# The opening of a hybrid decoder block: how x is normalised, turned and handed to the first projections

## Chip, cores, metric

One core of a Trainium2 chip. The metric is the device time of one execution in microseconds; the median of the runs is given. The hardware profiler recorded one further execution.

## What is computed

The reference is one pre-norm residual layer in float32 for 512 tokens of width 1024, with 16 learned meta tokens put in front (528 tokens in all). What matters here is its first step and what consumes it:

```python
def rmsnorm(x, g):
    y = x * rsqrt(mean(x * x, axis=-1) + 1e-6)
    return y * g

h = concatenate([zeros(PAD), meta_tokens, x])     # PAD only aligns blocks; masked out
u = rmsnorm(h, norm_g)
hq, hf, hi, hz, aq, ak, av, az, ga, gb = split(u @ w_in)   # ten 1024-wide projections
# branch A: gated linear recurrence on (hq, hf, hi), RMSNorm, silu(hz) gate
# branch B: differential softmax attention on (aq, ak, av), RMSNorm, silu(az) gate
m = sigmoid(ga) * (oA @ w_branch_a) + sigmoid(gb) * (oB @ w_branch_b)
out = rmsnorm(h + m @ w_out, final_g)             # meta tokens dropped
```

TensorE contracts over partitions, so `u` has to be brought into channel-major form (channels on the partitions, tokens in the columns) before the first projection. Matmuls of the projections are made of three products: each operand is split into a rounded high part (`_hi`, type fp32r) and the remainder (`_lo`), and hi·hi, hi·lo and lo·hi are summed in PSUM (function `three`, lines 379 to 383).

## The kernel before

x is taken in tiles of 128 tokens (0 to 3) and one tile of 16 meta tokens (index `CH` = 4), in the order `X_ORDER = (0, 1, CH, 2, 3)`. Each goes through these steps, and each step is a function called by hand in the program of its engine, so the order of the calls is the order of the work:

1. ScalarE squares it with a sum over the row (`square_x`, L717 to L724).
2. VectorE makes the mean plus eps (`mean_x`, L980), POOL raises it to −0.5 (L367): `rstd`.
3. VectorE multiplies the tile by `rstd` (one per token) and by the norm weight `g_in` in one instruction (`norm_x`, L977). `g_in` holds norm_g on all 128 partitions, a 512 KB broadcast.
4. TensorE turns its eight 128x128 blocks with the identity (`turn_x`, L386 to L401) into two PSUM banks.
5. ScalarE copies them out, rounded, to `uT_hi` (L734), and VectorE subtracts to get `uT_lo` (L996). The meta tile has shorter forms (L396, L730, L991).

Weights come in units of 128 output channels by 1024 (512 KB). A unit is loaded into one of two buffers, ScalarE makes its high part (`convert_hi`, L247) and VectorE its low part (`convert_lo`, L252); unit u is loaded once unit u−2 has been converted (`lo_ready`). The first two units are used in four pieces (`half_section`, L454): half 0 takes the meta tokens and tiles 0 and 1, half 1 tiles 2 and 3. 24 matmuls make one piece. `half_section(s, half)` waits for `lo_ready` of its unit and for `u_ready_lo`. Then come whole sections (`groups`), of which section 2, with 264-column matmuls, is the first. After them eight heads, each with its eight projections and its recurrence and attention laid between them, then gates, branch projections, the output projection and the last norm.

TensorE's order at the start: turn tiles 0 and 1, wait for `rows_ready` (three small loads into `rows_in`: lower-bound logits and two head norm weights) and transpose those 18 rows (L468), turn the meta tile and tile 2, half section (0,0), turn tile 3, half sections (1,0), (0,1), (1,1). VectorE waits for that transpose (`pe_pre`) and copies it (L1009) between its work on tiles 0 and 1.

DMAs are issued by SP (x tiles 0 and 1, weight unit 0, x tiles 2 and 3, unit 1, `rows_in`, four tables, then the further units) and by ScalarE (identity, norm_g, meta tokens). Engines work their queues in order, and wait on semaphores where shown.

Of the kernel before, what the change touches and what calls it, by code (L numbers as in the profile page):

```python
# [43 lines left out]

X_ORDER = (0, 1, CH, 2, 3)

# [46 lines left out]
def build(nc, x, meta_tokens, norm_g, w_in, lb_logits, hg_norm_g, da_lambda, da_norm_g,  # L93
# [22 lines left out]
    x_in, o2 = at("x_in", [P, NT, D], F32, region_o)  # L116
    g_in, o2 = at("g_in", [P, D], F32, o2)
    x_sq, o2 = at("x_sq", [P, D], F32, o2)
# [31 lines left out]
    gate_a, o = at("gate_a", [P, SEQ], F32, o)  # L150
    gate_b, o = at("gate_b", [P, SEQ], F32, o)
    kT, o = at("kT", [P, TOK], F32, o)
    qT, o = at("qT", [P, SEQ], F32, o)
# [31 lines left out]

    lbt = cols(2 * HEADS + 2)
    f_mul, f_neg, f_add, e_0, e_1, e_m = (cols(HEADS) for _ in range(6))
    gain_a, gain_b, neg_lam, lam2, warm = cols(1), cols(1), cols(1), cols(2), cols(NT)
    ss, ms, rstd, half_neg, ss2 = (cols(NT) for _ in range(5))
# [4 lines left out]
    def bank(i):  # L194
        return ps[:, i, :]
# [7 lines left out]
    def level_bank(e):  # L203
# [16 lines left out]
    x_squared, x_ms, x_rstd, x_normed, x_turned = (sem(n) for n in (  # L220
        "x_squared", "x_ms", "x_rstd", "x_normed", "x_turned"))

    sec_taken = sem("sec_taken")
# [61 lines left out]
    with block:  # L285

        @block.sync
        def _(sp):
# [89 lines left out]
        def _(pe):  # L378
# [6 lines left out]

            def turn_x(n):  # L386

                i = X_ORDER[n]
                pe.wait_ge(x_normed, n + 1)
                if i == CH:  # L390
                    pe.wait_ge(v_pre, 1)
                elif n > 2:
                    pe.wait_ge(u_ready_lo, n - 2)
                for k in range(KT):
                    if i == CH:
                        t = pe.transpose(bank(3)[:, k * META:(k + 1) * META], x_in[0:META, CH, k * P:(k + 1) * P],  # L396
                                         ident[0:META, 0:META])
                    else:
                        t = pe.transpose(bank(4 + 2 * (i % 2) + k // 4)[:, (k % 4) * P:(k % 4 + 1) * P],
                                         x_in[:, i, k * P:(k + 1) * P], ident[:, :])  # L400
                t.then_inc(x_turned, 1)  # L401


            def recurrent_out(s, b):
# [296 lines left out]
        @block.scalar  # L701
        def _(act):
            act.dma_start(ident[:, :], c_ident).then_inc(ident_in, 16)
            act.dma_start(g_in[:, :], norm_g.to_broadcast([P, D])).then_inc(norm_in, 16)
            act.dma_start(x_in[0:META, CH, :], meta_tokens).then_inc(meta_in, 16)

            act.wait_ge(g_pre, 1)
            act.activation(warm, half_neg, ACT.Square)

# [6 lines left out]

            def square_x(n):  # L717
                i = X_ORDER[n]
                m = P if i < CH else META
                act.wait_ge(*((x_loaded[i], 16) if i < CH else (meta_in, 16)))  # L720
                if n > 0:
                    act.wait_ge(x_squared, n)
                act.activation(x_sq[0:m, :], x_in[0:m, i, :], ACT.Square, accum_out=ss[0:m, i:i + 1]) \
                    .then_inc(x_squared, 1)  # L724

            def turned_x(n):
                i = X_ORDER[n]
                act.wait_ge(x_turned, n + 1)
                if i == CH:
                    act.activation(uT_hi[:, :, 0:META], bank(3)[:, 0:KT * META].rearrange("p (k t) -> p k t", k=KT),  # L730
                                   ACT.Copy).then_inc(u_ready_hi, 1)
                    return
                for g in range(2):
                    ins = act.activation(uT_hi[:, 4 * g:4 * g + 4, META + i * P:META + (i + 1) * P],  # L734
                                         bank(4 + 2 * (i % 2) + g).rearrange("p (k t) -> p k t", k=4), ACT.Copy)
                ins.then_inc(u_ready_hi, 1)
# [12 lines left out]
            turned_x(4)  # L749
            convert_hi(act, 2, 2, 2)  # L750
# [211 lines left out]
        def _(dve):  # L962
# [6 lines left out]

            def norm_x(n):  # L970

                i = X_ORDER[n]
                m = P if i < CH else META
                dve.wait_ge(x_rstd, n + 1)
                if n == 0:
                    dve.wait_ge(norm_in, 16)
                dve.scalar_tensor_tensor(x_in[0:m, i, :], x_in[0:m, i, :], rstd[0:m, i:i + 1], g_in[0:m, :],  # L977
                                         ALU.mult, ALU.mult).then_inc(x_normed, 1)

            def mean_x(n):  # L980
                i = X_ORDER[n]
                m = P if i < CH else META
                dve.wait_ge(x_squared, n + 1)
# [3 lines left out]
            def turned_x(n):  # L987
                i = X_ORDER[n]
                dve.wait_ge(u_ready_hi, n + 1)
                if i == CH:  # L990
                    dve.tensor_tensor(uT_lo[:, :, 0:META], bank(3)[:, 0:KT * META].rearrange("p (k t) -> p k t", k=KT),  # L991
                                      uT_hi[:, :, 0:META].bitcast(F32), ALU.subtract).then_inc(u_ready_lo, 1)
                    return
                for g in range(2):
                    lo, hi = (a[:, 4 * g:4 * g + 4, META + i * P:META + (i + 1) * P] for a in (uT_lo, uT_hi))
                    ins = dve.tensor_tensor(lo, bank(4 + 2 * (i % 2) + g).rearrange("p (k t) -> p k t", k=4),  # L996
                                            hi.bitcast(F32), ALU.subtract)
                ins.then_inc(u_ready_lo, 1)

            mean_x(0)  # L1000
            mean_x(1)
            norm_x(0)
            norm_x(1)
            mean_x(2)
            norm_x(2)
            turned_x(0)
            mean_x(3)
            dve.wait_ge(pe_pre, 1)
            pre(dve.tensor_copy(lbt, bank(3)[:, 256:256 + 2 * HEADS + 2]))  # L1009
            turned_x(1)  # L1010
            norm_x(3)
            convert_lo(dve, 0, 0)
            turned_x(2)
            mean_x(4)
            norm_x(4)
            turned_x(3)
            convert_lo(dve, 1, 1)
            turned_x(4)
            convert_lo(dve, 2, 2)
# [352 lines left out]
```

## Time and profile before

| | us |
|---|---|
| median of 3 runs (758.33 to 758.58) | 758.37 |
| the profiled execution | 758.68 |
| its span | 756.5 |

The profiled execution lasted 2.2 us longer than its span, which runs from the first to the last recorded activity. In the rows, PE is TensorE's matmuls, PEld its weight loads, DVE VectorE, ACT ScalarE, POOL GpSimd and SP the engine that issues DMAs; a q behind the name is the engine's sequencer. Start times are counted from the start of the span. "L381" is line 381 of the kernel.

### The profile page before, as it was taken

Reading aid. Unit: us, or ns where it says so; the run is one execution under the profiler, and the core shown is the slowest. Engines: PE = TensorE matmul, PEld = TensorE weight load, DVE = VectorE, ACT = ScalarE, POOL = GpSimd, SP = SyncE. Lnnn points to the kernel's source line nnn. Section 1 sums busy time; section 2 is a strip of 40 time slices with the busy share of each in tenths; the row PEclk is TensorE's granted clock in tenths of the full one; section 3 lists DMA queues with packets and bytes.
Section 4 is the critical chain, followed back from the end, with each engine's and each line's share of the span. In section 5 each row is a group of like instructions: output and inputs, shape, how many; then the busy total and the mean of one; then the engine's idle time right before and its main releaser. Section 6 shows DMA issues by size and latency. Waiting matters only on the chain.

```text
span 756.5 us, 13114 instructions
## 1 busy us (share of the span) xinstructions
PE 737.0 (97%) x4729; PEld 656.1 (87%) x4729; DVE 462.5 (61%) x973; ACT 284.0 (38%) x580; POOL 22.9 (3%) x34
## 2 busy tenths in 40 slices
PE   3999999999999999999999999999999999999996
PEld 2998999999899899989989989998888888888885
DVE  4668669668767856966876786695643433333352
ACT  5414443542552444255145235425522222232232
POOL 2000000000000000000000000000000000000001
PEclk9999999999999999999999999999999999999999
DMA  7421220230122123023012212302323223332602
GB/s 253 126 70 56 84 84 16 68 111 28 55 83 83 55 81 85 0 83 111 28 55 83 83 33 82 107 1 85 112 85 112 83 84 111 96 98 86 246 29 111
DMA packets 105416, 63.24 MB, mean 84 GB/s; under 512 B 2067, under 2 KB 100901, under 8 KB 105397
## 3 DMA queue, kind: packets, MB, share of 16 engines
q1 hardware_dynamic: 105076, 62.33, 27.4%
q10 hardware_dynamic: 320, 0.66, 0.3%
q8 instruction: 12, 0.20, 0.1%
q14 instruction: 8, 0.06, 0.0%
HBM read 60.88 MB, written 2.10 MB: 83 GB/s over the span
## 4 chain that ended last, share of the span: by engine, by line
PE 96%; SPq 1%; issue 1%; DMA 1%; DVE 0%; ACT 0%; POOLq 0%; POOL 0%; DVEq 0%; ACTq 0%
PE ps L381 26%; PE ps L382 26%; PE ps L383 26%; PE ps L502 3%; PE ps L571 3%; PE ps L600 2%; PE ps L488 1%; PE ps L591 1%; PE ps L578 1%; PE ps L601 1%; PE ps L536 1%; PE ps L535 1%; PE ps L518 1%; PE ps L543 1%; DMA rows_in<-in_da_norm_g 1%
## 5 line engine op out<-in xcount | busy, mean ns | idle before, releaser
L381 PE MATMUL ps<-uT_hi,w_hi 128*128 128x512 f32 (+3 forms) x960 | 323.9, 337 | 0.0
L382 PE MATMUL ps<-uT_lo,w_hi 128*128 128x512 f32 (+3 forms) x960 | 308.6, 321 | 0.0
L383 PE MATMUL ps<-uT_hi,w_lo 128*128 128x512 f32 (+3 forms) x960 | 308.0, 321 | 0.0
L383 PEld LDWEIGHTS ps<-uT_hi,w_lo 128*128 128x128 f32 x960 | 181.0, 189 | 13.9
L381 PEld LDWEIGHTS ps<-uT_hi,w_hi 128*128 128x128 f32 x960 | 181.8, 189 | 12.1
L382 PEld LDWEIGHTS ps<-uT_lo,w_hi 128*128 128x128 f32 x960 | 181.7, 189 | 11.1
L252 DVE TENSOR_TENSOR w_lo<-w_raw,w_hi 128x1024 fp32r<-128x1024 f32 x104 | 126.2, 1220 | 95.9 <-ACT w_hi L247 95.1
L247 ACT ACTIVATE w_hi<-w_raw 128x1024 fp32r<-128x1024 f32 x104 | 110.0, 1057 | 87.5 <-PE ps L383 84.3
L809 ACT ACTIVATE e<-ps,small 128x144 f32<-128x144 f32 (+2 forms) x48 | 23.0, 483 | 47.7 <-DVE small L1194 47.7
L1140 DVE TENSOR_REDUCE small<-sq 128x4 f32<-128x512 f32 x16 | 11.0, 686 | 40.1 <-ACT sq L798 40.1
L371 POOL TENSOR_TENSOR small<-small 128x4 f32<-128x4 f32 x16 | 16.1, 1007 | 512.5 <-DVE small L1141 512.5
L502 PE MATMUL ps<-qq,sq 128*128 128x128 f32 x192 | 29.9, 278 | 0.0
L502 PEld LDWEIGHTS ps<-qq,sq 128*128 128x128 f32 x192 | 27.1, 190 | 3.0
L1131 DVE COPY_PREDICATED aa<-masks,ps 128x256 f32<-128x256 uint8 x56 | 29.0, 518 | 0.0
L1191 DVE TENSOR_REDUCE small<-ps 128x2 f32<-128x288 f32 (+3 forms) x32 | 26.9, 841 | 0.0
L834 ACT ACTIVATE kT_hi<-kT 128x528 fp32r<-128x528 f32 x8 | 5.2, 646 | 57.5 <-DVE kT L1177 57.5
L381 PE MATMUL ps<-oa_hi,w_hi 128*128 128x512 f32 x64 | 24.9, 390 | 0.0
L382 PE MATMUL ps<-oa_lo,w_hi 128*128 128x512 f32 x64 | 24.9, 389 | 0.0
L383 PE MATMUL ps<-oa_hi,w_lo 128*128 128x512 f32 x64 | 24.9, 389 | 0.0
L381 PE MATMUL ps<-ob_hi,w_hi 128*128 128x512 f32 x64 | 24.9, 389 | 0.0
L382 PE MATMUL ps<-ob_lo,w_hi 128*128 128x512 f32 x64 | 24.9, 389 | 0.0
L383 PE MATMUL ps<-ob_hi,w_lo 128*128 128x512 f32 x64 | 24.9, 389 | 0.0
(191 smaller groups left out, 1020.4 us busy)
## 6 DMA issues: line engine op xcount, KB each, us to landing
w_raw<-in_w_in SPq DMA_DIRECT2D x80, 512.0 KB, 3.7
w_raw<-in_w_branch_a SPq DMA_DIRECT2D x8, 512.0 KB, 3.5
w_raw<-in_w_branch_b SPq DMA_DIRECT2D x8, 512.0 KB, 3.6
w_raw<-in_w_out SPq DMA_DIRECT2D x8, 512.0 KB, 3.9
x_in<-in_x SPq DMA_DIRECT2D x4, 512.0 KB, 7.8
x_res<-in_x SPq DMA_DIRECT2D x4, 512.0 KB, 6.4
out<-y_out SPq DMA_DIRECT2D x8, 256.0 KB, 2.2
rope<-in_c_rope SPq DMA_DIRECT2D x1, 528.0 KB, 6.0
```

Of the source, the lines that this page charges most:

```text
L247: act.activation(w_hi[:, slot, :], w_raw[:, slot % RAW, :], ACT.Copy).then_inc(hi_ready, 1)
L252: eng.tensor_tensor(w_lo[:, slot, :], w_raw[:, slot % RAW, :], w_hi[:, slot, :].bitcast(F32), ALU.subtract).then_inc(lo_ready, 1)
L371: pool.tensor_tensor(rstd[:, 0:CH], ms[:, 0:CH], half_neg[:, 0:CH], ALU.pow).then_inc(rstd_ready, 1)
L381: pe.matmul(dst, w[0], rhs[0], start=start, stop=False, skip_group_check=True)
L382: pe.matmul(dst, w[0], rhs[1], start=False, stop=False, skip_group_check=True)
L383: return pe.matmul(dst, w[1], rhs[0], start=False, stop=stop, skip_group_check=True)
L502: mm = pe.matmul(walk(dst, i * P // 2, (P, 2), (m, P // (2 * m)), (1, m)), k_mix[:, i, :], walk(qq[:, i * P:], m, (HALF - m, 2), (2 * m, P ...
L571: pe.matmul(bank(B_S + comp)[:, 0:n - at_k], q[half[comp], q_b], k[half[comp], at_k:n], start=i == 0, stop=False, skip_group_check=True)
L600: pe.matmul(dst, pT[:, j, :], v_b[:, j, :], start=(j == 0), stop=False)
L809: ins = act.activation(e[:, 0:n], bank(B_S + comp)[:, 0:n], ACT.Exp, bias=nb[:, comp:comp + 1], scale=SCALE, accum_out=lsum[:, comp:comp + 1])
L1131: dve.copy_predicated(dst, mask, got).then_inc(lvl_taken, 1)
L1191: chain(dve.tensor_reduce(mx, ps[:, B_S:B_S + 2, 0:n], AX.X, ALU.max))
```

## The change

- `X_ORDER` becomes `(CH, 0, 1, 2, 3)`: the meta tile is first. Its squares are taken by VectorE instead of ScalarE (`meta_sq`, with the sum).
- `g_in` holds norm_g on 16 partitions only (64 KB), for the meta tile, which is still multiplied by `rstd` and norm_g in one instruction. For all other tiles norm_g is applied later: it is also loaded as 8 rows of 128 (`g_rows`, 4 KB), transposed by TensorE and copied to the 8 columns `g_col`, and used as the per-partition scale when PSUM is copied out, by ScalarE (`scale=g_col`) and by VectorE (a SCALAR_TENSOR_TENSOR in place of the TENSOR_TENSOR). Both norm_g loads are issued by SP behind x1; ScalarE issues meta first, then the identity.
- Tiles 0 and 1 are not normalised on VectorE. VectorE multiplies the identity by `rstd` into a diagonal matrix (128x128), and TensorE multiplies the raw block with this diagonal, an fp32 matmul in place of a transpose. Tiles 2 and 3 are still multiplied by `rstd` on VectorE (a TENSOR_SCALAR) and transposed with the identity.
- PSUM is laid out by channel block: two tiles (256 columns) of two k share a bank, and PSUM is copied out in pieces of 256 columns, two k at a time, with a semaphore count for each pair.
- TensorE's order: ten matmuls of a zero tile with itself (`WARM`), the transpose of norm_g, diagonal turn of tile 0, meta turn, diagonal turn of tile 1, half section (0,0), turns of tiles 2 and 3, half section (1,0), transpose of `rows_in`, half sections (0,1) and (1,1).
- The zero tile, the diagonals and `g_rows` lie in buffers that the heads use later.

The core of the diff:

```diff
-X_ORDER = (0, 1, CH, 2, 3)
+X_ORDER = (CH, 0, 1, 2, 3)
+WARM = 10
...
                 if i == 1:
+                    sp.dma_start(g_rows, norm_g.rearrange("l (k p) -> (l k) p", p=P)).then_inc(g_loaded, 16)
+                    sp.dma_start(g_in[:, :], norm_g.to_broadcast([META, D])).then_inc(norm_in, 16)
                     section(0, 0, 0, 0)
...
+            pool.memset(zeros, 0.0).then_inc(zeros_ready, 1)
             pool.memset(half_neg, -0.5).then_inc(g_pre, 1)
...
+            def scale_and_turn(i):
+                pe.wait_ge(diag_ready, i + 1)
+                for k in range(KT):
+                    mm = pe.matmul(turned(k, i), x_in[:, i, k * P:(k + 1) * P], diag[:, i, :], start=True, stop=True)
+                    if i == 1 and k % 2 == 1:
+                        mm.then_inc(x_turned, 1)
+
+            def turn_x(i):
+                pe.wait_ge(x_normed, i)
+                for k in range(KT):
+                    if i == 2:
+                        pe.wait_ge(u_ready_lo, k // 2 + 1)
+                    t = pe.transpose(turned(k, i), x_in[:, i, k * P:(k + 1) * P], ident[:, :])
+                    if i == 3 and k % 2 == 1:
+                        t.then_inc(x_turned, 1)
...
             def half_section(s, half):
                 pe.wait_ge(lo_ready, s + 1)
-                pe.wait_ge(u_ready_lo, (3, NT)[half])
+                pe.wait_ge(u_ready_lo, (4, 8)[half])
...
+            pe.wait_ge(zeros_ready, 1)
+            for _ in range(WARM):
+                pe.matmul(bank(2)[:, P:2 * P], zeros, zeros, start=True, stop=True)
             pe.wait_ge(ident_in, 16)
-            turn_x(0)
-            turn_x(1)
+            pe.wait_ge(g_loaded, 16)
+            pe.transpose(bank(2)[:, 0:KT], g_rows, ident[0:KT, 0:KT]).then_inc(g_turned, 1)
+            scale_and_turn(0)
+            turn_meta()
+            scale_and_turn(1)
+            half_section(0, 0)
+            turn_x(2)
+            turn_x(3)
+            half_section(1, 0)
             pe.wait_ge(rows_ready, 48)
             pe.transpose(bank(3)[:, 256:256 + 2 * HEADS + 2], rows_in[:, :], ident[0:2 * HEADS + 2, 0:2 * HEADS + 2]) \
                 .then_inc(pe_pre, 1)
-            turn_x(2)
-            turn_x(3)
-            half_section(0, 0)
-            turn_x(4)
-            half_section(1, 0)
             half_section(0, 1)
             half_section(1, 1)
...
+            def turned_hi(half):
+                for j in range(KT // 2):
+                    act.wait_ge(x_turned, KT // 2 * half + j + 1)
+                    for k in (2 * j, 2 * j + 1):
+                        ins = act.activation(uT_hi[:, k, META + half * HALF:META + (half + 1) * HALF],
+                                             ps[:, 4 + j, k % 2 * HALF:(k % 2 + 1) * HALF], ACT.Copy,
+                                             scale=g_col[:, k:k + 1])
+                    ins.then_inc(u_ready_hi, 1)
             square_x(0)
             square_x(1)
+            convert_hi(act, 0, 0, 1)
+            meta_turned_hi()
+            act.wait_ge(g_ready, 1)
+            turned_hi(0)
             square_x(2)
-            turned_x(0)
             square_x(3)
-            turned_x(1)
-            convert_hi(act, 0, 0, 1)
-            turned_x(2)
-            square_x(4)
-            turned_x(3)
             convert_hi(act, 1, 1, 1)
-            turned_x(4)
+            turned_hi(1)
             convert_hi(act, 2, 2, 2)
...
+            def diagonal(i):
+                dve.wait_ge(x_rstd, i + 2)
+                dve.tensor_scalar(diag[:, i, :], ident[:, :], rstd[:, i:i + 1], None, ALU.mult).then_inc(diag_ready, 1)
...
+            dve.wait_ge(meta_in, 16)
+            meta_x = x_in[0:META, CH, :]
+            dve.scalar_tensor_tensor(meta_sq[:, :], meta_x, 1.0, meta_x, ALU.mult, ALU.mult,
+                                     accum_out=ss[0:META, CH:CH + 1]).then_inc(meta_squared, 1)
             mean_x(0)
+            dve.wait_ge(g_turned, 1)
+            dve.tensor_copy(g_col, bank(2)[:, 0:KT]).then_inc(g_ready, 1)
+            dve.wait_ge(norm_in, 16)
+            dve.wait_ge(x_rstd, 1)
+            dve.scalar_tensor_tensor(meta_x, meta_x, rstd[0:META, CH:CH + 1], g_in[:, :], ALU.mult, ALU.mult) \
+                .then_inc(x_normed, 1)
+            dve.wait_ge(ident_in, 16)
             mean_x(1)
+            diagonal(0)
             mean_x(2)
+            diagonal(1)
+            convert_lo(dve, 0, 0)
+            dve.wait_ge(meta_hi, 1)
+            dve.tensor_tensor(uT_lo[:, :, 0:META], bank(3)[:, 0:KT * META].rearrange("p (k t) -> p k t", k=KT),
+                              uT_hi[:, :, 0:META].bitcast(F32), ALU.subtract)
+            dve.wait_ge(g_ready, 1)
+            turned_lo(0)
+            mean_x(3)
+            norm_x(2)
+            mean_x(4)
+            norm_x(3)
+            convert_lo(dve, 1, 1)
+            turned_lo(1)
             dve.wait_ge(pe_pre, 1)
             pre(dve.tensor_copy(lbt, bank(3)[:, 256:256 + 2 * HEADS + 2]))
```

## Rows read from the trace of the kernel before

**Rows 1.** The page: busy time, granted clock in 40 slices, one group of section 5

```profile
PE 737.0 (97%) x4729; PEld 656.1 (87%) x4729; DVE 462.5 (61%) x973; ACT 284.0 (38%) x580; POOL 22.9 (3%) x34
...
PEclk9999999999999999999999999999999999999999
...
PE 96%; SPq 1%; issue 1%; DMA 1%; DVE 0%; ACT 0%; POOLq 0%; POOL 0%; DVEq 0%; ACTq 0%
...
L252 DVE TENSOR_TENSOR w_lo<-w_raw,w_hi 128x1024 fp32r<-128x1024 f32 x104 | 126.2, 1220 | 95.9 <-ACT w_hi L247 95.1
```

**Rows 2.** Timeline of TensorE: start us, us, engine, line, operation, count [idle before]

```profile
9.83 3.65 PE L399 MATMUL ps<-ident,x_in 128*128 128x128 f32 x16 [9.83 <-DVE x_in L977]
15.21 0.29 PE L468 MATMUL ps<-ident,rows_in 18*128 18x18 f32 x1 [1.73 <-DMA rows_in<-in_da_norm_g]
15.86 1.00 PE L396 MATMUL ps<-ident,x_in 16*128 16x16 f32 x8 [0.36 <-DVE small L1009]
18.15 1.97 PE L399 MATMUL ps<-ident,x_in 128*128 128x128 f32 x8 [1.29 <-DVE x_in L977]
19.77 0.58 PE L381 MATMUL ps<-uT_hi,w_hi 128*128 128x272 f32 x1
20.15 0.43 PE L382 MATMUL ps<-uT_lo,w_hi 128*128 128x272 f32 x1
...
22.60 0.28 PE L381 MATMUL ps<-uT_hi,w_hi 128*128 128x272 f32 x1
...
24.11 1.04 PE L399 MATMUL ps<-ident,x_in 128*128 128x128 f32 x8
...
33.51 0.28 PE L381 MATMUL ps<-uT_hi,w_hi 128*128 128x264 f32 x1
```

**Rows 3.** Chain of waits in order of time: start us, us, what

```profile
4.89 4.42 SPq L308
...
9.73 5.43 DMA rows_in<-in_da_norm_g
...
52.86 0.45 PE ps L502 x4
```

**Rows 4.** Timeline of ScalarE, square of tile 0

```profile
4.68 1.06 ACT L723 ACTIVATE x_sq<-x_in 128x1024 f32<-128x1024 f32 x1 [1.02 <-DMA x_in<-in_x]
5.64 0.19 ACT L723 ACTIVATION_READ_ACCUMULATOR x_sq<-x_in 128x1 f32 x1
```

**Rows 5.** Stretches: window, its length, engines' busy us, clock, DMA share, GB/s

```profile
10.50:12.00 1.50, 1.50 (x9) 1.40 (x9) 0.96 (x2) 0.20 (x1) 0.46 (x1) 1.00 1.01 387
```

**Rows 6.** DMA issues to 60 us: KB each, median us from issue to landing

```profile
w_raw<-in_w_in SPq DMA_DIRECT2D x9, 512.0 KB, 3.7
...
g_in<-in_norm_g ACTq DMA_DIRECT2D x1, 512.0 KB, 7.0
```

**Rows 7.** Timeline of VectorE: the meta tile's mean and norm, the copy of rows_in

```profile
11.33 0.13 DVE L984 TENSOR_SCALAR small<-small 16x1 f32<-16x1 f32 x1
12.11 1.27 DVE L977 SCALAR_TENSOR_TENSOR x_in<-x_in,small,g_in 16x1024 f32<-16x1024 f32 x1 [0.65 <-POOL small L367]
...
15.53 0.18 DVE L1009 COPY small<-ps 128x18 f32<-128x18 f32 x1 [0.89 <-PE ps L468]
```

**Rows 8.** Groups by form, ScalarE and VectorE: busy us, mean ns | idle before

```profile
L786 ACT ACTIVATE z_g<-ps,small 128x512 f32<-128x512 f32 x16 | 10.8, 673 | 0.0
L785 ACT ACTIVATE th_z<-ps 128x512 f32<-128x512 f32 x16 | 9.3, 584 | 40.4 <-PE ps L383 40.4
L823 ACT ACTIVATE pT<-ps 128x256 f32<-128x256 f32 x8 | 3.1, 383 | 1.9 <-PE ps L594 1.9
L1105 DVE TENSOR_TENSOR kk<-kk,tt 128x256 f32<-128x256 f32 x40 | 17.0, 424 | 11.1 <-PE ps L502 8.1 <-DVE e L1173 1.5 <-DVE e L1166 1.5
L1205 DVE TENSOR_SCALAR e<-e,small 128x528 f32<-128x528 f32 x8 | 3.9, 490 | 0.0
L1205 DVE TENSOR_SCALAR e<-e,small 128x144 f32<-128x144 f32 x8 | 2.3, 288 | 0.0
```

More of the change, by code:

```diff
@@ L116, in build @@
     x_in, o2 = at("x_in", [P, NT, D], F32, region_o)
-    g_in, o2 = at("g_in", [P, D], F32, o2)
+    g_in, o2 = at("g_in", [META, D], F32, o2)
+    meta_sq, o2 = at("meta_sq", [META, D], F32, o2)
     x_sq, o2 = at("x_sq", [P, D], F32, o2)
@@ L151, in build @@
     gate_b, o = at("gate_b", [P, SEQ], F32, o)
+    diag, zeros, g_rows = st[:, 0:2, :], on[:, 0, :], og[0:KT, 0:P]
     kT, o = at("kT", [P, TOK], F32, o)
@@ L184, in cols @@
         return small[:, taken[0] - n:taken[0]]
-    lbt = cols(2 * HEADS + 2)
+    lbt, g_col = cols(2 * HEADS + 2), cols(KT)
     f_mul, f_neg, f_add, e_0, e_1, e_m = (cols(HEADS) for _ in range(6))
-    gain_a, gain_b, neg_lam, lam2, warm = cols(1), cols(1), cols(1), cols(2), cols(NT)
+    gain_a, gain_b, neg_lam, lam2, warm = cols(1), cols(1), cols(1), cols(2), cols(1)
     ss, ms, rstd, half_neg, ss2 = (cols(NT) for _ in range(5))
@@ L221, in build @@
         "x_squared", "x_ms", "x_rstd", "x_normed", "x_turned"))
+    zeros_ready, g_loaded, g_turned, g_ready = (sem(n) for n in ("zeros_ready", "g_loaded", "g_turned", "g_ready"))
+    meta_squared, meta_turned, meta_hi, diag_ready = (sem(n) for n in (
+        "meta_squared", "meta_turned", "meta_hi", "diag_ready"))
     sec_taken = sem("sec_taken")
@@ L383, in three, with turn_meta, turned @@
                 return pe.matmul(dst, w[1], rhs[0], start=False, stop=stop, skip_group_check=True)
[L386 to L393, printed above, removed]
-                for k in range(KT):
[L395 to L401, printed above, removed]
+            def turn_meta():
+                pe.wait_ge(x_normed, 1)
+                for k in range(KT):
+                    t = pe.transpose(bank(3)[:, k * META:(k + 1) * META], x_in[0:META, CH, k * P:(k + 1) * P],
+                                     ident[0:META, 0:META])
+                t.then_inc(meta_turned, 1)
+            def turned(k, i):
+                return ps[:, 4 + k // 2, (k % 2) * HALF + (i % 2) * P:(k % 2) * HALF + (i % 2 + 1) * P]
+            def scale_and_turn(i):
[12 more added lines that the diff above has]
+                        t.then_inc(x_turned, 1)
             def recurrent_out(s, b):
@@ L702, in _ @@
         def _(act):
+            act.dma_start(x_in[0:META, CH, :], meta_tokens).then_inc(meta_in, 16)
             act.dma_start(ident[:, :], c_ident).then_inc(ident_in, 16)
-            act.dma_start(g_in[:, :], norm_g.to_broadcast([P, D])).then_inc(norm_in, 16)
-            act.dma_start(x_in[0:META, CH, :], meta_tokens).then_inc(meta_in, 16)
             act.wait_ge(g_pre, 1)
-            act.activation(warm, half_neg, ACT.Square)
+            act.activation(warm, half_neg[:, 0:1], ACT.Square)
             act.sem_inc(og_ready, 2)
@@ L715, in _, with square_x @@
             act.sem_inc(gate_taken, 4)
[L717 to L736, printed above, removed]
+            def square_x(i):
+                act.wait_ge(x_loaded[i], 16)
+                if i > 0:
+                    act.wait_ge(x_squared, i)
+                act.activation(x_sq[:, :], x_in[:, i, :], ACT.Square, accum_out=ss[:, i:i + 1]).then_inc(x_squared, 1)
@@ new lines, in meta_turned_hi @@
+            def meta_turned_hi():
+                act.wait_ge(meta_turned, 1)
+                act.activation(uT_hi[:, :, 0:META], bank(3)[:, 0:KT * META].rearrange("p (k t) -> p k t", k=KT),
+                               ACT.Copy).then_inc(meta_hi, 1)
+            def turned_hi(half):
[6 more added lines that the diff above has]
+                    ins.then_inc(u_ready_hi, 1)
@@ L968, in pre @@
                 return own[0]
[L970 to L978, printed above, removed]
             def mean_x(n):
@@ L982, in mean_x @@
                 m = P if i < CH else META
-                dve.wait_ge(x_squared, n + 1)
+                dve.wait_ge(*((x_squared, n) if n else (meta_squared, 1)))
                 dve.tensor_scalar(ms[0:m, i:i + 1], ss[0:m, i:i + 1], 1.0 / D, EPS, ALU.mult, ALU.add) \
                     .then_inc(x_ms, 1)
[L987 to L998, printed above, removed]
@@ L1000, in _, with norm_x, turned_lo @@
-            mean_x(0)
+            def diagonal(i):
+                dve.wait_ge(x_rstd, i + 2)
+                dve.tensor_scalar(diag[:, i, :], ident[:, :], rstd[:, i:i + 1], None, ALU.mult).then_inc(diag_ready, 1)
+            def norm_x(i):
+                dve.wait_ge(x_rstd, i + 2)
+                dve.tensor_scalar(x_in[:, i, :], x_in[:, i, :], rstd[:, i:i + 1], None, ALU.mult) \
+                    .then_inc(x_normed, 1)
+            def turned_lo(half):
+                for j in range(KT // 2):
+                    dve.wait_ge(u_ready_hi, KT // 2 * half + j + 1)
+                    for k in (2 * j, 2 * j + 1):
+                        lo, hi = (a[:, k, META + half * HALF:META + (half + 1) * HALF] for a in (uT_lo, uT_hi))
+                        ins = dve.scalar_tensor_tensor(lo, ps[:, 4 + j, k % 2 * HALF:(k % 2 + 1) * HALF],
+                                                       g_col[:, k:k + 1], hi.bitcast(F32), ALU.mult, ALU.subtract)
+                    ins.then_inc(u_ready_lo, 1)
@@ L1005, in _ @@
+            mean_x(3)
             norm_x(2)
-            turned_x(0)
-            mean_x(3)
+            mean_x(4)
+            norm_x(3)
+            convert_lo(dve, 1, 1)
+            turned_lo(1)
             dve.wait_ge(pe_pre, 1)
             pre(dve.tensor_copy(lbt, bank(3)[:, 256:256 + 2 * HEADS + 2]))
[L1010 to L1017, printed above, removed]
@@ L1018, in _ @@
-            turned_x(4)
             convert_lo(dve, 2, 2)
```

3 lines of the change are left out of this document (1 added, 2 removed).

## The prediction

> **What bounds the kernel now.** I read the page first: TensorE is busy in 97% of the span, and the chain that ended last lies 96% on it [rows 1]. The other engines wait for it, so the only time to be won or lost by an edit of the opening is the time at which TensorE begins its unbroken run, and the rate at which it starts. I therefore went to the timeline of TensorE [rows 2]. The reader is to see four stretches there: nothing until 9.83; 16 transposes to 13.48; a hole until 15.21, which the transpose of rows_in ends; then small pieces until 18.15, from which it never stops again. The first weight matmul starts at 19.77, and the groups of section 2 (the first 264-column one) at 33.51. From there on both kernels have the same instructions, so I forecast the shift of this one moment. The chain of waits [rows 3] says why the hole is there: rows_in was issued late, its first DMA held SP for 4.42 us, and the last landed 5.43 us after issue. Behind that wait stood two more turns on TensorE and the copy on VectorE.
>
> The rate is the second thing. The page grants full speed in every slice (a 9, [rows 1]), and still the 272-column matmuls start every 0.223 us from 20.15 to 22.60 (eleven steps, the last already shorter), and every 0.126 us from 22.60 to 24.11 (twelve). 272 columns in 0.223 us is the 1.2 GHz level, in 0.126 us the 2.4 GHz level. The granted clock of the profile does not show this step; the pitch does. The 16 transposes at 9.83 (0.228 us each) ran at the low level too; the eight at 24.11 took half as long (1.04 for 1.97 us).
>
> **The opening after the change.** Loads first. SP issues x0, x1, then the two small norm_g loads (4 KB and 64 KB), and the 512 KB broadcast of norm_g is gone from ScalarE's queue. x0 was used at 4.68 [rows 4]. At 387 GB/s [rows 5] the 0.52 MB of x1 take 1.35 us more, so x1 is there near 6.0, and norm_g right behind, say 6.1. That is the first term: **norm_g at 6.1.** The bounds: 5.7, if meta and ident fit in earlier, and, by the 7.0 us from issue to landing of the old broadcast [rows 6] on an issue at 1.6, 8.6.
>
> TensorE's zero matmuls start after POOL's first memset, about 1.0. An fp32 128-column matmul is two records here: the chain has four records of L502 in 0.45 us [rows 3], 0.225 us a matmul at the high level, double at the low one. Ten take 4.5 us, to 5.5 at the latest, before norm_g is there: they cost nothing. Nor do the other edits of the first 6 us, all of them under the loads: one memset more on POOL, the squares of the meta tile on VectorE (1.27 [rows 7] and a power, from some 3.7 to 5.8), one DMA issue less on ScalarE; without that cover the squares would add 1.3. Then the queue of VectorE decides, because it is in order and mean_x of x0 stands behind the whole meta norm:
> - transpose of norm_g and its copy, as those of rows_in from 15.21 [rows 2] to 15.53 + 0.18 [rows 7]: 0.5 together, to 6.6;
> - meta norm, one instruction of 1.27, at 12.11 [rows 7]: 7.85;
> - mean, power on POOL, next instruction: 0.78, from 11.33 to 12.11 [rows 7]: 8.65. The other edges of this step (x0 squared near 5.9) are long done;
> - the diagonal, 128 columns, no row of its own; the 144-column TENSOR_SCALAR takes 0.29 [rows 8]: scale_and_turn(0) starts at **8.9**.
>
> TensorE then has 8 fp32 matmuls in place of 8 transposes: 1.8 us at the high level, to 10.7. The eight meta transposes took 1.00 at 15.86, taken unchanged: 11.7. scale_and_turn(1): 1.8, to 13.5, with the first pair of k handed on at 12.15. The diagonal for x1 and lo(0) lie on VectorE meanwhile (0.78 + 0.3, then 1.22 [rows 1], from 8.8 to 11.1), the weights' hi on ScalarE after x1's square; both are covered, by more than 0.5 us.
>
> Now the evictions are the bound, not TensorE (0.45 a pair). The 256-column activation out of PSUM takes 0.383, and I take starts to overlap by 0.1; a per-partition scale adds 0.09 (0.673 with, 0.584 without, at 512 columns, [rows 8]). That is 0.36 to 0.37 a start, so 0.72 a pair, four pairs: 12.15 to 15.05. VectorE's two 256-column operations (0.424 each, 0.35 apart [rows 8], a tensor pair standing for the new form) follow the last pair: 0.8. Half section (0,0) starts at **15.9**; bounds 14.9 (0.28 a start and g at 5.7) and 18.4 (g at 8.6).
>
> The sum to the start of section 2, against 19.77 to 33.51 of before:
> - first weight matmul 15.9 for 19.77: −3.9;
> - its 24 matmuls at 0.126, 3.0 us, for 4.34 (19.77 to 24.11): −1.3, if the clock is up;
> - two turns of x stand behind it, where there was one: +0.9;
> - rows_in's transpose, now within the run: +0.3.
> Together −4.0.
>
> Does the second half keep up? ScalarE after 15.05: two squares with their accumulator reads (4.68 to 5.83, 1.15 each [rows 4]), hi(1) of the same size 1.06: 18.4. VectorE: mean and power 0.78 after the first square, 17.0; norm_x(2) now is a TENSOR_SCALAR. 144 columns take 0.288 and 528 take 0.490, 0.53 ns a column [rows 8], so 1024 make 0.75 (an estimate), not the 1.27 of the norm of before [rows 7]: 17.75; the same once more: 19.2; lo(1) 1.22: 20.4. TensorE needs x3 at 19.8 and lo(1) at 20.7: covered by 0.6 and 0.3. The four pairs of x2 and x3 then run on ScalarE from 20.0 to 22.9 and on VectorE to 23.7, and TensorE asks for them at 23.8. That is a tie; I add 0.2 for it. **−3.8 us.** If norm_x took 1.27 after all, 0.8 more would be lost here, net of the cover of 0.3 to 0.6: I keep that for the range. Later, w2 to w6 are asked for by lo_ready, which moves with the rest.
>
> The profiled execution took 758.68 for a span of 756.5, and the median of the runs is 758.37. −3.8 gives 754.9 against the profiled execution and 754.6 against the median; I forecast 754.6, 0.5% faster.
>
> **A rule that speaks against this.** The rows [rows 2] show TensorE at the low level after an idle opening, and show one rise, at 22.5, after unbroken work from 18.15; no row shows a fall, because there is no idle stretch later. In the new order it stands still, but for one small transpose, from 5.5 to 8.9, and again from 13.5 to 15.9. The Trainium skill (TensorE: Matmul & The Clock Gate, section on the HAM clock gate) says that the engine goes back to half rate when left idle, so that warming up early can be lost by the time the data is there. No row shows it. If it holds here, rival 1 is the case.
>
> **Rivals.**
> 1. *The clock is low where it counts.* The zeros do not raise it, or the wait until 8.9 loses it. Then scale_and_turn(0) takes 3.65, to 12.55, the meta turn is done at 13.55, and if the rise comes 4.35 us after 8.9, as from 18.15, scale_and_turn(1) is fast: first pair 14.0, half section at 17.7, 1.8 later: −2.0, 756.4. With a rise after 2.7 us, as counted from the first weight matmul at 19.77, it would be −2.4. If it is lost between 13.5 and 15.9 instead, the 1.3 us of the half section are not won: −2.5. For it: the two idle stretches. Against: the zero matmuls last as long (4.5) as the run that raised it before.
> 2. *norm_g lands late as well:* 1.5 us later (7.6) and the clock low: −0.5, 757.9. This is "no change". For it: the spread of the landings, where 512 KB took 3.7 us in the median of the weights and 7.0 in the opening [rows 6].
> 3. *Slower: the gate on norm_g.* Before, norm_g was needed by one instruction; now VectorE's whole queue stands behind g_turned, x0's power included. A tiny load is not a quick one: rows_in went from 4.89 to 15.16, 10.3 us [rows 3]. If norm_g issued at 1.6 lands at 11.9, everything is 5.8 us later, 2.0 us net, and with the clock low (TensorE idle since 5.5) 3.8: 760.4 to 762.2. It decides from a landing at 9.9. Against: rows_in stood behind four tiles of x and two weight units and a DMA that held SP, norm_g stands behind x0 and x1 only.
>
> **How the numbers follow.** Forecast 58%, rival 1 25%, rival 2 10%, rival 3 7%. A measurement of this kernel can tell about 0.2%, 1.5 us, from no change. Faster: the forecast, and nearly all of rival 1, 0.81; same: rival 2 and a rest, 0.13; slower: 0.06. The range: below, 753.6 (the first bound, 14.9, for 15.9); above, 757.0, which holds rival 1 and a g at 7.6 with the clock up.
>
> **What would show it.** TensorE's timeline: zeros from 1.0 to about 5 with a pitch that halves before their end; L502-like pitch of 0.11 a record in the scaled turns, from 8.9; first weight matmul at 15.9 with a pitch of 0.126 from the start; the first 264-column matmul at 29.7; no idle time of TensorE afterwards beyond 0.3. A scaled turn at 0.22 a record speaks for rival 1, a VectorE copy of norm_g after 7.5 for rivals 2 and 3. I am wrong if TensorE idles elsewhere in the opening, above all ahead of half section (1,0) or (0,1), or if section 2 starts 3 us earlier and the time does not follow.

## The result and the profile after

The change made the kernel slower. Median 760.43 us (759.67 to 762.51, 11 runs) against 758.58 us of the kernel before in the same runs (758.02 to 759.25): ratio 1.0029, 95% interval 1.0021 to 1.0037. That is 1.85 us by the medians. The forecast was 754.6 with a range of 753.6 to 757.0. The profiled execution has a span of 758.4 (756.5 before): +1.9.

The page after, as in [rows 1]: TensorE is as dominant as before.

```profile
PE 743.3 (98%) x4766; PEld 662.0 (87%) x4766; DVE 462.6 (61%) x984; ACT 284.9 (38%) x586; POOL 22.1 (3%) x35
...
PE 96%; DVE 1%; issue 1%; DMA 1%; ACT 0%; POOL 0%; SPq 0%; POOLq 0%; DVEq 0%; ACTq 0%
```

The timeline of TensorE after, which answers to [rows 2] (single 272-column matmuls thinned out; `on`, `st` and `og` are the buffers that are lent to the zero tile, the diagonals and `g_rows`):

```profile
1.00 4.64 PE L484 MATMUL ps<-on 128*128 128x128 f32 x20 [1.00 <-POOL on L367]
7.28 0.24 PE L487 MATMUL ps<-ident,og 8*128 8x8 f32 x1 [1.64 <-DMA og<-in_norm_g]
10.01 3.78 PE L409 MATMUL ps<-st,x_in 128*128 128x128 f32 x16 [2.49 <-DVE st L999]
13.72 0.71 PE L398 MATMUL ps<-ident,x_in 16*128 16x16 f32 x8
14.36 2.05 PE L409 MATMUL ps<-st,x_in 128*128 128x128 f32 x16
19.48 0.36 PE L390 MATMUL ps<-uT_hi,w_hi 128*128 128x272 f32 x1 [3.07 <-DVE uT_lo L1011]
...
20.69 0.42 PE L390 MATMUL ps<-uT_hi,w_hi 128*128 128x272 f32 x1
20.91 0.43 PE L391 MATMUL ps<-uT_lo,w_hi 128*128 128x272 f32 x1
...
24.08 1.93 PE L418 MATMUL ps<-ident,x_in 128*128 128x128 f32 x16
25.76 0.36 PE L390 MATMUL ps<-uT_hi,w_hi 128*128 128x256 f32 x1
...
29.64 0.35 PE L390 MATMUL ps<-uT_hi,w_hi 128*128 128x256 f32 x1 [0.63 <-DVE uT_lo L1011]
...
35.39 0.28 PE L390 MATMUL ps<-uT_hi,w_hi 128*128 128x264 f32 x1
```

The first 264-column matmul starts at 35.39, 1.88 later than at 33.51: the whole loss, and nothing behind it adds to it. The reader is to see three things. The first scaled turn (L409, 16 records) takes 3.7 us and the second, of the same instructions, about 1.9 (3.78 and 2.05 with the last record's tail): between them TensorE's rate doubled. The half section starts 3.07 us after the turns are done, waiting for VectorE. And its matmuls start every 0.125 us until 20.69 and every 0.23 afterwards: the rate was lost again. Stretches of TensorE (length, busy, granted clock, DMA share, GB/s):

```profile
10.00:15.00 5.00, 4.99 (x29) 1.00 1.08 356
15.00:20.00 5.00, 1.93 (x17) 1.00 0.36 96
20.00:25.00 5.00, 5.00 (x31) 0.66 0.07 19
```

0.66 is a mean of the two levels, 2.4 and 1.2 GHz. The low level of 10.01 to 13.7 is not in the column (1.00); only the pitch of the records shows it.

VectorE's and ScalarE's timeline after, for [rows 7] and [rows 4]:

```profile
7.55 0.17 DVE L1021 COPY small<-ps 128x8 f32<-128x8 f32 x1 [2.11 <-PE ps L487]
7.66 1.27 DVE L1024 SCALAR_TENSOR_TENSOR x_in<-x_in,small,g_in 16x1024 f32<-16x1024 f32 x1
8.86 0.13 DVE L994 TENSOR_SCALAR small<-small 128x1 f32<-128x1 f32 x1
9.67 0.28 DVE L999 TENSOR_SCALAR st<-ident,small 128x128 f32<-128x128 f32 x1 [0.67 <-POOL small L376]
...
16.11 3.23 DVE L1011 SCALAR_TENSOR_TENSOR uT_lo<-ps,small,uT_hi 128x256 fp32r<-128x256 f32 x8 [1.04 <-ACT uT_hi L755]
```

```profile
15.17 3.02 ACT L755 ACTIVATE uT_hi<-ps,small 128x256 fp32r<-128x256 f32 x8 [0.43 <-PE ps L409]
```

The chain of waits after, for [rows 3]: the landing of norm_g and, twice, the eight evictions of VectorE lie on it.

```profile
1.66 5.48 DMA og<-in_norm_g
...
16.11 3.24 DVE uT_lo L1011 x8
...
26.26 3.24 DVE uT_lo L1011 x8
```

The DMA issues after, to 20 us (KB each, median us from issue to landing), for [rows 6]:

```profile
ident<-in_c_ident ACTq DMA_DIRECT2D x1, 64.0 KB, 5.7
g_in<-in_norm_g SPq DMA_DIRECT2D x1, 64.0 KB, 5.3
```

The identity was issued at 1.20, so it is there at 6.9. norm_g's rows landed at 7.14 and let TensorE go at 7.28.

The loss has three candidates: **clock** (TensorE at 1.2 GHz in the scaled turns and in the half section), **gate** (x0's mean and diagonal stand in VectorE's queue behind norm_g and the meta norm), **evictions** (3.07 us in series with the matmuls).

### The profile page after: what moved, and what is told of

Same layout as the page of the kernel before. It is cut to its first block, busy times and chain, and to the rows that moved or that the text cites. A ratio compares the mean times of both kernels' runs of the same rounds, so it can differ in the third digit from the quotient of the medians.

```text
span 758.4 us, 13207 instructions
## 1 busy us (share of the span) xinstructions
PE 743.3 (98%) x4766; PEld 662.0 (87%) x4766; DVE 462.6 (61%) x984; ACT 284.9 (38%) x586; POOL 22.1 (3%) x35
## 4 chain that ended last, share of the span: by engine, by line
PE 96%; DVE 1%; issue 1%; DMA 1%; ACT 0%; POOL 0%; SPq 0%; POOLq 0%; DVEq 0%; ACTq 0%
PE ps L390 26%; PE ps L391 25%; PE ps L392 25%; PE ps L525 3%; PE ps L594 3%; PE ps L623 2%; PE ps L511 1%; PE ps L614 1%; PE ps L601 1%; PE ps L624 1%; PE ps L559 1%; PE ps L558 1%; PE ps L541 1%; PE ps L566 1%; DVE uT_lo L1011 1%
```

## The experiments

All edits are to the changed kernel if not said otherwise; `zeros(n)` stands for n zero matmuls like those of `WARM`. Ratios are against the kernel before in the same runs.

**e1: no zeros.**

```diff
-WARM = 10
+WARM = 0
```

> The changed kernel with WARM = 0, nothing else. Theory C (the clock: the ten zero matmuls end at 5.64 and had not raised TensorE's rate when the scaled turns began at 10.01): the zeros do nothing, so the time stays that of the changed kernel, 760.4 within 0.5; the scaled turn of tile 0 is slow in both. Rival G (the zeros do help somewhere, for instance by letting the rise come earlier): 1 to 2 us more, 761.5 to 762.5.

760.61 (ratio 1.0031, 1.0022 to 1.0040). The zeros of the change do nothing: the first scaled turn took 3.79 without them, 3.78 with them.

**e2: zeros in one gap.**

```diff
             scale_and_turn(1)
+            zeros(13)
             half_section(0, 0)
```

> The changed kernel with 13 more zero matmuls in the gap between the scaled turn of tile 1 (ends 16.4) and half section (0,0) (starts 19.48). Theory C: the rate fell at 20.6 because TensorE stood idle for 3.07 us; filled, the 24 matmuls of half section (0,0) take 3.0 us and not 4.6, the two turns behind them up to 0.8 less: 2.2 us gained against the changed kernel, about 758.2, and no stretch of low granted clock after 20. Rival W (what counts are the waits on VectorE, the clock costs little): TensorE is released no earlier, the gain turns into a wait before the next piece, under 0.7 us gained.

760.36 (1.0013, 1.0003 to 1.0023; 758.17 to 761.11): in the median the expected 2.2 did not come. But the eleven runs fall into two groups: five lie at 758.2 to 759.0, 1.4 to 2.3 below the median of the changed kernel, whose fastest run is 759.67, and six at 760.4 to 761.1. The profiled execution is of the second group (760.79), and shows why nothing is gained there. Both scaled turns ran at the low level, and so did the first zeros. VectorE had its last pair at 20.55, and the zeros kept TensorE until 21.65:

```profile
14.98 3.78 PE L409 MATMUL ps<-st,x_in 128*128 128x128 f32 x16
18.55 3.34 PE L492 MATMUL ps<-on 128*128 128x128 f32 x26
21.65 0.37 PE L390 MATMUL ps<-uT_hi,w_hi 128*128 128x272 f32 x1
```

This filling of fixed length came too late where the rate was low when it started; my expectation took the moment of the rise from one profile. That the rate was already up when the zeros of those five runs began is my reading; none of the five was profiled.

**e3: zeros in all gaps.**

```diff
-WARM = 10
+WARM = 14
...
+            zeros(6)      # behind the transpose of norm_g
             scale_and_turn(0)
...
             scale_and_turn(1)
+            zeros(13)
             half_section(0, 0)
```

> The changed kernel with zeros in all gaps of the opening: 14 at the start, 6 behind the transpose of norm_g, 13 before half section (0,0). Theory C: the scaled turn of tile 0 runs at the high rate, 1.8 us and not 3.8, half section (0,0) starts near 17.4, and its 24 matmuls take 3.0: about 3.9 us gained against the changed kernel, 756.5, that is 2 us faster than the kernel before. Rival W: as for the filling of one gap alone, since the chain over VectorE sets the starts: less than 1.5 us gained.

756.99 (0.9977, 0.9968 to 0.9986), and all ten runs within 756.87 to 757.15. 3.4 us against the changed kernel, 3.9 expected. With its clock restored the change is thus 1.7 us faster than the kernel before, by the ratio. The scaled turn begins where it did, and from there on everything runs at the high level:

```profile
9.96 2.05 PE L409 MATMUL ps<-st,x_in 128*128 128x128 f32 x16 [0.95 <-DVE st L1003]
...
17.66 0.36 PE L390 MATMUL ps<-uT_hi,w_hi 128*128 128x272 f32 x1 [0.17 <-DVE uT_lo L1015]
20.76 1.91 PE L418 MATMUL ps<-ident,x_in 128*128 128x128 f32 x16
```

**e4: tile 0 ahead of norm_g on VectorE** (g copy and meta norm moved behind the two diagonals).

> The changed kernel with VectorE's queue in another order: means and diagonals of tiles 0 and 1 first, the copy of norm_g and the norm of the meta tile behind. Theory W (the gate on norm_g and the meta norm holds the scaled turns): they start at about 7.6, not 10.01, since the identity is there at 6.9. With the low rate until a rise near 13 the half section starts 1.2 to 2.0 us earlier: 758.4 to 759.2. Theory C alone: TensorE is idle longer behind its scaled turns, the rate falls all the same, and what is won by the order is lost again: within 0.5 of 760.4.

757.24 (0.9978, 0.9969 to 0.9987). 3.2 us gained, more than the 1.2 to 2.0 expected. The first scaled turn starts at 7.38, 2.6 earlier, and in the profiled execution the half section starts at 16.64, 2.8 earlier. The gate holds TensorE; how much of it is clock, this run can't say.

**e5: waits by pair.**

```diff
-                pe.wait_ge(u_ready_lo, (4, 8)[half])
                 for k in range(KT):
+                    if k % 2 == 0:
+                        pe.wait_ge(u_ready_lo, 4 * half + k // 2 + 1)
```

> The changed kernel with one edit: a half section waits for each pair of channel blocks just before it uses it, not for all four pairs at its start. Theory V (the idle 3.07 us ahead of half section (0,0) are the evictions, in series with the matmuls only because of the single wait): TensorE starts on the first pair near 17.1, so the idle stretch is about 0.8 us, the rate does not fall afterwards, and half section (0,0) ends near 20.2 and not 24.1. The turn of tile 2 then waits for VectorE until 20.8 and that of tile 3 until 22.3. All in all 3 us gained against the changed kernel: 757.4. Rival: the clock falls anyway, in the small gaps that the pairs leave (0.05 us each): 1.5 us gained, 758.9.

757.61 (0.9986, 0.9977 to 0.9995), 2.8 us against the changed kernel, 3 expected. TensorE's idle stretch shrinks to 0.72 and no stretch behind it is at the low level. Again two causes went at once: the serial evictions, and the fall of the rate. The first scaled turn still took 3.78.

**e15, e16: gate and evictions at a fixed clock.** e15 is e3 with the waits of e5 in place of the 13 zeros. e16 is e3 with tile 0's mean and diagonal, and tile 1's mean, ahead of the copy of norm_g, in place of the 6 zeros.

> Zeros at the start (14) and behind the transpose of norm_g (6), so that the scaled turns run at the high rate, and waits by pair in place of the filling before half section (0,0). Against e3_fill_both (757.0), which has the same clock and the single wait, the difference is the evictions in series alone. If they cost by themselves: half section (0,0) starts at 15.3 and not 17.7, the turn of tile 3 waits for VectorE until 20.5, the idle 0.63 ahead of half section (0,1) goes: 1.4 us gained, 755.6. If only the clock made them dear: 756.7 to 757.0.

> Zeros at the start (14) and before half section (0,0) (13), and VectorE's queue with tile 0's mean and diagonal ahead of norm_g. Against e3_fill_both (757.0), same clock, the difference is the gate on norm_g alone. Theory W: scaled turn of tile 0 at 7.4 and not 10.0, half section (0,0) at 15.1 and not 17.7, all of it kept: 754.5. If VectorE's later work (norms of tiles 2 and 3) takes it back: 755.5 or more.

755.53 (755.35 to 755.80; 0.9957, 0.9943 to 0.9970) and 754.70 (754.47 to 754.98; 0.9946, 0.9932 to 0.9959), both within 0.2 of the expectation. In both profiles the scaled turns and half section (0,0) run at the high level, as in e3. So at the high rate the evictions in series cost 757.0 − 755.5 = 1.5 us and the gate 757.0 − 754.7 = 2.3 us.

**e6: everything together.** e16's order on VectorE, waits by pair, 14 zeros at the start, 6 behind half section (0,0).

> All that the runs so far point to, in the changed kernel: means and diagonal of tile 0 ahead of the copy of norm_g, waits by pair, 14 zero matmuls at the start instead of 10, and 6 behind half section (0,0). If the losses (gate on norm_g 2.6, evictions in series 3, clock 2) are independent parts: first scaled turn at 7.4, section 2 near 28 to 29.5, 753 to 754.5. If they overlap, so that the last one left (VectorE: low parts, then norms of tiles 2 and 3) holds TensorE: 755 to 756.5.

752.92 (752.87 to 753.17; ratio 0.9923, 0.9910 to 0.9937): 5.8 us faster than the kernel before, 7.5 than the changed one. The three parts add up: 760.4 − 3.4 − 1.5 − 2.3 = 753.2 (the 6 zeros behind half section (0,0) were not tried alone). Its TensorE, with VectorE's diagonal of tile 0:

```profile
7.00 0.28 DVE L1002 TENSOR_SCALAR st<-ident,small 128x128 f32<-128x128 f32 x1 [0.75 <-DMA ident<-in_c_ident]
7.37 0.20 PE L488 MATMUL ps<-ident,og 8*128 8x8 f32 x1 [1.50 <-DMA og<-in_norm_g]
7.49 2.05 PE L409 MATMUL ps<-st,x_in 128*128 128x128 f32 x16
9.47 0.66 PE L398 MATMUL ps<-ident,x_in 16*128 16x16 f32 x8
10.07 2.05 PE L409 MATMUL ps<-st,x_in 128*128 128x128 f32 x16
12.85 0.36 PE L390 MATMUL ps<-uT_hi,w_hi 128*128 128x272 f32 x1 [0.72 <-DVE uT_lo L1014]
...
28.19 0.28 PE L390 MATMUL ps<-uT_hi,w_hi 128*128 128x264 f32 x1
```

Two landings now set the start: the diagonal waited for the identity, and the scaled turn started 0.12 behind the transpose of norm_g, which waited for its rows (0.14 in e4, 0.12 in e16).

**e14: e6 without any zeros.**

> The best version so far without any zero matmul. If warming up is worth its own gain only once TensorE has no long idle stretches behind it: first scaled turn at the low rate, 3.8 us for 2.0, and part of the second too, 1.6 to 3 us slower than 752.9, 754.5 to 756, with a wider spread. If it is worth nothing here either, as in the changed kernel: 752.9 within 0.4.

755.78 (754.82 to 756.11; 0.9960, 0.9946 to 0.9973), 2.9 slower than e6. Both scaled turns took 3.8. Zeros at the start were worth nothing in the changed kernel (e1) and zeros are worth 2.9 us here. The two are not quite the same: e1 takes out 10, e14 takes out 14 at the start and 6 behind half section (0,0). 14 zeros with the gaps left open were not run, so how much of the difference is the number of zeros is not shown.

**e11, e13: the diagonal undone**, in the changed kernel and in e6.

```diff
-mm = pe.matmul(turned(k, i), x_in[...], diag[:, i, :], start=True, stop=True)
+mm = pe.transpose(turned(k, i), x_in[...], ident[:, :])
-dve.tensor_scalar(diag[:, i, :], ident[:, :], rstd[:, i:i + 1], None, ALU.mult)
+dve.tensor_scalar(x_in[:, i, :], x_in[:, i, :], rstd[:, i:i + 1], None, ALU.mult)
```

> The changed kernel with the diagonal undone: tiles 0 and 1 are normalised by VectorE in place (0.75 each for 0.28) and turned by transposes (0.11 or 0.23 each) in place of fp32 matmuls (0.23 or 0.46). If the diagonal helps as it saves 0.47 us twice on VectorE: 0.5 slower, 760.9. If it hurts since its matmul takes two passes more: the first turn ends 1.4 us earlier while the rate is low, the second 0.5 to 1.4, half section (0,0) starts 1.5 to 2 us earlier: about 758.7. If transposes do not bring TensorE's rate up, half section (0,0) then runs at the low rate from its start, and what is won is given back: 760.

759.50 (1.0013, 1.0004 to 1.0022), 0.9 faster than the changed kernel; the two intervals just touch. The eight transposes of a tile take 1.97 at the low level where the fp32 matmuls took 3.78. In its profile the rate stays low all the way from 10 to 20 (granted 0.50, pitch 0.23), and half section (0,0), at 18.82, starts at the low level: the third case of the expectation, with half a microsecond more won than it said.

> The best version so far (all edits, 752.9) with the diagonal undone: VectorE normalises tiles 0 and 1, TensorE transposes. At the high rate the diagonal costs 0.9 us a tile on TensorE and saves 0.47 a tile on VectorE, and VectorE's pairs set the pace: 0.5 slower than 752.9, 753.4. If TensorE's passes set it: 0.9 faster, 752.0.

754.87 (753.08 to 754.93; 0.9942, 0.9928 to 0.9955), 1.9 slower than e6. Two of five runs are at 753.1 and 753.2 with a mean granted clock of 0.998 or 0.999, three at 754.9 with 0.994. I read this as 0.2 for the order by itself and 2.0 where the rate falls. In the profile, one of the three, it is granted 0.50 from about 10 to 17; the two at 753 have no profile. Whether the gaps left by the shorter transposes bring the fall about, or the transposes themselves, is not shown. The mean clock alone is a weak witness: the three slowest runs of e1 (762.1 to 762.2) have 0.998, others of its runs at 760.3 have 0.995.

**e12: small loads first.** Identity ahead of meta on ScalarE's queue, both norm_g loads ahead of x1.

> The changed kernel with another order of loads: identity ahead of the meta tokens on ScalarE's queue, both norm_g loads ahead of x1 on SP's. Theory W (the landing of identity and norm_g, 6.9 and 7.2, sets VectorE's queue): copy of norm_g near 5.7, first scaled turn near 8.2 and not 10.0; 1 to 1.9 us gained against the changed kernel, 758.5 to 759.4. Rival: small loads land late wherever they stand, or x1 lands as much later: within 0.5 of 760.4.

760.85 (1.0038, 1.0024 to 1.0052): no gain, as the rival said, though not for its reason alone. norm_g was turned at 5.91, 1.4 earlier, but the meta tokens came at 5.99 in place of 4.05, and their squares stand first in VectorE's queue:

```profile
5.99 1.21 DVE L1018 SCALAR_TENSOR_TENSOR meta_sq<-x_in 16x1024 f32<-16x1024 f32 x1 [5.99 <-DMA x_in<-in_meta_tokens]
...
7.32 0.14 DVE L1022 COPY small<-ps 128x8 f32<-128x8 f32 x1
8.21 1.27 DVE L1025 SCALAR_TENSOR_TENSOR x_in<-x_in,small,g_in 16x1024 f32<-16x1024 f32 x1 [0.74 <-POOL small L377]
```

**e8, e9: single parts in the kernel before.** e8 moves rows_in's transpose and copy behind half section (1,0); e9 adds 24 zeros at the start, 10 ahead of the transpose of rows_in and 5 behind the meta turn.

> The kernel before with one part of the change alone: the transpose of rows_in and VectorE's copy of it stand behind half section (1,0). By the chain of waits of the kernel before, everything behind 15.21 comes about 1.5 us earlier, and the transpose costs 0.3 within the run: 1.2 us gained against the kernel before, if the rate rises as much earlier; if the rise stays where it was, 0.6. Rival: VectorE sets the start of half section (0,0) anyway (it has norm, low parts and lo(0) in a row): within 0.4 of the kernel before.

758.01 (0.9995, 0.9986 to 1.0004): not told apart from the kernel before, where 1.2 or 0.6 had been expected. The half section starts at 19.05, 0.7 earlier, but TensorE is idle for 3.35 us before the turn of tile 2 and is then at the low level until about 23.

> The kernel before with zero matmuls and nothing else: 24 at the start, 10 ahead of the transpose of rows_in, 5 behind the meta turn. If the clock can be had without the new opening: the turn of tile 2 ends 0.9 earlier, half section (0,0) takes 3.0 us and not 4.3, but VectorE (lo(0), meta low part, lo(1)) holds the starts at 19.5 and 23.8: 1.1 us gained, 757.6. If VectorE and rows_in hold TensorE wholly: within 0.4 of the kernel before.

758.69 (1.0002, 0.9993 to 1.0011): no gain where 1.1 was expected, though two of the eleven runs lie at 757.2 and 757.3. In the profile the rate was up for the turn of tile 0 (1.06) and down again for that of tile 1 (1.97). The ten zeros behind it ran at the low level until about 15.3, took 3.19 us in all, and the transpose of rows_in came behind them, at 16.82 for 15.21.

**e17: the changed kernel once more.**

> The changed kernel once more, unedited, for a second profile. If the moments at which TensorE's rate rises and falls are not tied to the program, the zero matmuls, the scaled turns and half section (0,0) show other lengths than 4.64, 3.78 and 4.60 us, and the span differs by up to 2 us from 758.4. If they are tied to it, the rows repeat within 0.2.

Span 758.4 again (one run, 760.30), but the first scaled turn took 3.46, not 3.78: the rate rose before its end. Across kernels it is plainer. Five of the profiles begin with the same 28 records of zeros, seven with the same 20, and TensorE has nothing ahead of them:

| | length of the zeros |
|---|---|
| 28 records: e3, e13, e16, e6, e15 | 6.23, 6.10, 5.12, 4.87, 4.77 |
| 20 records: changed kernel, e17, e12, e2, e11, e5, e4 | 4.64, 4.64, 4.63, 4.62, 4.25, 3.88, 3.85 |

20 records at the low level make 4.6; a shorter run had the rise within it. The moment is not tied to the program. In e4, e5 and e11 the zeros did raise the rate, and the idle stretch up to the data lost it again (granted 0.50 from 7.3 in e4 and e5, from 8.1 in e11).

## Why the prediction was wrong

By its own steps, for the profiled execution:

| step | forecast | measured | adds |
|---|---|---|---|
| norm_g copied (landed: 6.1, measured 7.14) | 6.6 | 7.72 | +1.1 |
| from there to the first scaled turn | 2.3 | 2.29 | 0 |
| first scaled turn | 1.8 | 3.71 | +1.9 |
| meta turn | 1.0 | 0.64 | −0.4 |
| second scaled turn to half section (0,0) | 4.2 | 5.12 | +0.9 |
| half section (0,0) | 3.0 | 4.60 | +1.6 |
| two turns | 1.8 | 1.68 | −0.1 |
| the rest to section 2 | 9.0 | 9.63 | +0.6 |
| section 2 starts | 29.7 | 35.39 | +5.7 (parts rounded) |

**The step that failed is "1.8 us at the high level" for the first scaled turn, and with it "if the clock is up" in the half section.** Together +3.5 of the 5.7 in the profile, 3.4 by e3. I had the mechanism as rival 1 at 25%, but as an either-or: the rate low at the scaled turns (−2.0) or lost before the half section (−2.5). Both happened: it was low in the first scaled turn, rose before the second, and fell again behind the idle 3.07 us, 1.2 us into the half section. The fall stands in all four profiles that have this gap behind a raised rate (changed kernel, e17, e1, e4), and in neither e3, where the gap is 0.17, nor e5, where it is 0.72. Against rival 1 I had held that the zeros last as long as the run that raised the rate before. That was one profile's length taken for a rule. The same zeros raised the rate in some executions and not in others. Where they did, TensorE then stood idle for 2.4 to 2.9 us, and the first scaled turn was at the low level all the same (e4, e5, e11); taking the zeros out changed nothing (e1). The rule of the Trainium skill that I had weighed (TensorE: Matmul & The Clock Gate, HAM clock gate: the engine goes back to half rate when left idle) is the case here: granted 0.66 in 20 to 25, with the pitch doubling at 20.7. The remark of the Trainium skill in the same section of that page that the moment of the change varies between runs, by half a microsecond either way, agrees in kind. Here it varied more: the same 28 records took 4.77 to 6.23 us. I should have read it as a reason to give the clock less than even odds, since by my own sum the new order left TensorE idle for 3.4 us between the zeros and their use, and for 2.4 us ahead of the half section.

**norm_g landed 1.0 late; the gate behind it was priced right.** The landing was forecast at 6.1 with 5.7 to 8.6 as bounds; it came at 7.14, the identity at 6.9. The chain behind it took 2.29 for 2.3. The order of VectorE's queue was in that sum; what I did not ask is what another order would give: 2.3 us at a fixed clock, with tile 0 first (e16). e12 shows that moving norm_g's load ahead is no gain while the meta tokens then come 1.9 later. It does not show that the landings don't matter: with tile 0 first they are what TensorE waits for (e6).

**The evictions were mis-sized by 0.9.** ScalarE's pitch was right (eight in 3.02, 0.36 from start to start). VectorE's was not: its new form took 0.39 from start to start, 3.23 for eight, against 0.35, so VectorE set the pace and ended 1.15 behind ScalarE, not 0.8. ScalarE took up the first pair 0.81 after the start of the turn, not 0.45. That the evictions stand in series with the matmuls was in the sum as it should be; waiting by pair takes 1.5 us of it away at a fixed clock (e15).

**The second half was no tie (+0.4 of the +0.6).** TensorE idled 0.63 us ahead of half section (0,1), where I had allowed 0.2. The prediction had named idle time at this place as a sign of being wrong. It is VectorE's slower pitch again: its eight evictions from 26.26 to 29.5 stand in the chain.

**Right:** the loss or gain lies wholly ahead of section 2; the meta turn, half section (1,0) and the norms of tiles 2 and 3 did not hold TensorE (norm_x 0.75 measured, 0.75 estimated).

**What the rivals were worth.** The measured 760.4 is the lower end of rival 3's range (760.4 to 762.2), by luck: its landing at 9.9 or later did not happen. Nearest is rival 2, norm_g late and the clock low: the landing was 1.0 late for its 1.5, and its sign, a copy of norm_g after 7.5, came (7.55). It forecast 757.9, since it had the low clock at one place only. With the clock restored e3 measures 756.99, still 2.4 above the forecast, of which the other rows of the table make 2.1 (+1.1, +0.9 and +0.6, less 0.5 for the turns).

What stays open: how much of the changed kernel's spread (759.7 to 762.5) is the rise and how much the fall; the runs give a mean clock, not the two moments.

## What to carry to other kernels

Before warming TensorE up, list its idle stretches between the warm-up and the first long run: 10 zeros were worth nothing with the stretches open, 20 were worth 2.9 us once they were closed. Close a stretch first by releasing the matmuls piece by piece as their operands come (1.5 us by the wait alone), and put the work that TensorE waits for ahead of anything else in an in-order queue (2.3 us). When an engine's rate depends on its past, price an edit at both rates and with the spread of runs. The four versions whose profile has the high rate from the first scaled turn to section 2 (e3, e6, e15, e16) repeat within 0.3 to 0.5 us, the other edits of the changed kernel within 1.3 to 2.9.

## What the runs showed of the hardware

- The moment at which TensorE's rate rises is not tied to the program: 28 identical records from 1.00 took between 4.77 and 6.23 us (e15, e3), and one program had its first scaled turn in 3.78 and in 3.46 (changed kernel, e17).
- The granted clock of the profile can read 1.00 while the pitch is that of 1.2 GHz. In each case it had not yet changed in that trace (changed kernel, 10 to 13.7; e14, both scaled turns of 3.8 us). Behind a first change it read 0.50 at the same pitch (e2, 10 to 15).
- Eight 128-column fp32 matmuls took 3.7 us at the low level and about 1.9 at the high one, eight transposes 1.97 and 1.04 to 1.09: here a product with a diagonal cost twice a transpose.
- The identity, 64 KB, took 5.7 us to land when issued at 1.20 behind the meta tokens (changed kernel). Issued first it took 4.8 in the changed kernel (e12) and 4.1 in the kernel before.
